# First layer's norm factor applied to products, its inputs split straight from x

## The chip, the cores and the metric

The kernel runs on one core of a Trainium2 chip. The metric is the device time of one execution in microseconds (us). Three runs of the kernel before took 2198.29, 2200.40 and 2200.71 us; the median is 2200.4 us.

## The reference

One layer of a recurrent mixer (with a gated embedding) is followed by one layer that joins a convolution branch, a bidirectional gated recurrence and an MLP. There are 256 tokens of width 2048. The part that matters here is the head of the first layer:

```
def _rmsnorm(x, g):
    xf = x.astype(jnp.float32)
    y = xf * lax.rsqrt(jnp.mean(xf * xf, axis=-1, keepdims=True) + NORM_EPS)
    return (y * g.astype(jnp.float32)).astype(x.dtype)

    u = _rmsnorm(h, norm_pre[i])
...
    proj = u @ w_in
    xb, gate = proj[..., :LRU_WIDTH], proj[..., LRU_WIDTH:]
    xc = conv_general_dilated(xb, conv_w, ...) + conv_b      # 4 taps, causal
    r = sigmoid(einsum(xblk, w_r) + b_r);  i = sigmoid(einsum(xblk, w_i) + b_i)
...
    y = h.astype(u.dtype) * jax.nn.silu(gate)
    return y @ w_out
```

The factor of the norm, `rsqrt(mean(x*x) + eps)`, is one number per token. It is the same for all 2048 features that a product sums over, so it can stand before the product or behind it. The gain `g` is one number per feature and has to stand before it.

## The kernel before, in words

Activations lie with the features on the 128 partitions and the 256 tokens along the row: x is 16 tiles of 128x256. A weight matrix comes as blocks of 128x1024 (512 KB); SyncE loads them in the order of use into a ring of 7 slots, `WF`. Every product is made of three matmuls, so that it keeps f32 precision: ScalarE writes the rounded block, `WH` (a step `high`), VectorE writes what is left, `WL` (a step `low`), and the moving side `SR` is split in the same way. `WH` and `WL` have four slots each: `high` of block n waits until block n-4 has been used. A block is 24 matmuls of 256 columns. Block 0 is the first one that is used; blocks 0 to 7 belong to the first four tiles of the first layer's input projection ("xb" 0 to 3, built side by side, `linear_quad`), and each later tile takes two blocks (`linear`).

All engines walk one list of steps made by `timetable` (L56 to L495); each engine takes from it the steps that concern it, in that order, and waits on semaphores in between. `prepare` puts the `high` steps three blocks (`LA`) ahead of use; a `low` follows at the beginning of the next block. `evac` takes a finished tile out of its PSUM bank (four banks go round), and `after` steps come one, two or three block beginnings later, as the table `AFTER` says. `bg` steps are parts of background work (`small_params`, `recurrence`), one behind every second product.

The start: SyncE loads the parameters (332 KB) and constants, the four pieces of x (512 KB each), then the weights. ScalarE squares the pieces of x, VectorE sums them, TensorE adds over the partitions by a product with ones (`stat`), ScalarE takes the root, VectorE the reciprocal (step `recip`). Only then is x multiplied by gain and factor and split (`normed`, a step `make` for each of the 16 tiles of x).

An xb tile leaves PSUM thus: ScalarE writes it, scaled by the last of the four convolution taps, into `XCf` (L1091), then VectorE adds the other three taps straight from PSUM (L1518 to L1526), and the third of them frees the bank. `after` 1 and 2 split the result for the gates. Tiles of "gates" (sigmoid on ScalarE), and 16 tiles "gate" follow.

Among the weight blocks stand blocks of another matrix, `mod`. The 24 that `add_spread` places are used by TensorE directly, two matmuls of 512 columns each (`modp`), and need neither `high` nor `low`. 14 of them stand among the xb tiles and 10 among the gate tiles. In the middle of the xb tiles VectorE turns masks loaded by DMA into bytes (step `late`).

## Time and profile before

| | before |
|---|---|
| median of three runs | 2200.4 us |
| the profiled execution | 2203.85 us |
| its span, first to last instruction | 2202.1 us |
| mean granted TensorE clock | 0.991 |
| TensorE busy | 2134.1 us (97%) |
| VectorE busy | 1586.3 us (72%) |
| ScalarE busy | 1006.8 us (46%) |
| GpSimd busy | 64.1 us (3%) |

The profiled execution took 3.5 us more than the median. The span leaves out what lies before the first and behind the last instruction, 1.75 us. TensorE is busy for nearly all of the span, so what counts is the time in which it stands still or runs at the lower clock; most of what concerns the change lies in the first 160 us.

### The profile page before, as it was taken

How to read it: one execution, taken by the hardware profiler on the slowest of the kernel's cores; microseconds unless marked ns; L12 is line 12 of the kernel's file. 1: busy time of each engine (PE TensorE's matmuls, PEld its weight loads, DVE VectorE, ACT ScalarE, POOL GpSimd, SP SyncE). 2: the span in 40 equal slices, each digit the busy share in tenths (PEclk: the TensorE clock that was granted, in tenths of full speed). 3: DMA queues.
4: the chain of work that ended last, by engine and by line, in shares of the span. 5: the costliest groups of instructions: out<-in, count | busy, mean ns of one | idle time of the engine just before them, and what ended most of it. 6: DMA issues, size and time to landing. Idle time of an engine off the chain costs nothing.

```text
span 2202.1 us, 34105 instructions
## 1 busy us (share of the span) xinstructions
PE 2134.1 (97%) x14048; PEld 1910.2 (87%) x14048; DVE 1586.3 (72%) x2365; ACT 1006.8 (46%) x1494; POOL 64.1 (3%) x61
## 2 busy tenths in 40 slices
PE   6999999999999999999999999989999999999997
PEld 5877899798988888999999999968888888888885
DVE  6757788588879876567777788776766766656655
ACT  5667444455632322445544444444444434434443
POOL 0000002020000000000000000100000000000011
PEclk9999999999999999999999999999999999999998
DMA  6556777676743466434436988936775675555552
GB/s 227 192 185 203 247 233 274 211 259 210 252 140 124 131 222 240 143 120 127 131 125 198 350 290 297 326 125 199 249 255 185 220 240 192 180 191 191 183 181 87
DMA packets 121691, 447.96 MB, mean 203 GB/s; under 512 B 13504, under 2 KB 13760, under 8 KB 121152
## 3 DMA queue, kind: packets, MB, share of 16 engines
q1 hardware_dynamic: 121536, 445.78, 60.1%
q8 instruction: 111, 1.82, 0.3%
q14 instruction: 44, 0.36, 0.1%
HBM read 441.53 MB, written 4.19 MB: 202 GB/s over the span
## 4 chain that ended last, share of the span: by engine, by line
PE 68%; DVE 4%; ACT 1%; issue 0%; DVEq 0%; ACTq 0%
PE bank L767 67%; DVE AR L1385 1%; DVE WL L1385 1%; DVE AR L1472 1%; DVE AR L1392 1%; DVE SR L1392 0%; PE bank L887 0%; ACT AR L1024 0%; ACT AR L1023 0%; ACT L1024 0%; PE bank L918 0%; ACT WH L1023 0%; ACT SR L1024 0%; DVE SR L1385 0%; ACT SR L1023 0%
## 5 line engine op out<-in xcount | busy, mean ns | idle before, releaser
L767 PE MATMUL bank<-SR,WH 128*128 128x256 f32 (+1 forms) x8128 | 1945.8, 325 | 29.1 <-DVE WL L1385 10.4
L767 PEld LDWEIGHTS bank<-SR,WH 128*128 128x128 f32 x8128 | 1363.5, 191 | 184.6 <-issue 31.0
L767 PE MATMUL bank<-SR,WL 128*128 128x256 f32 (+1 forms) x5088 | 1479.9, 291 | 0.0
L767 PEld LDWEIGHTS bank<-SR,WL 128*128 128x128 f32 x5088 | 972.5, 191 | 14.9
L1385 DVE TENSOR_TENSOR WL<-WF,WH 128x1024 fp32r<-128x1024 f32 x636 | 772.0, 1225 | 218.5 <-ACT WH L1023 218.0
L1023 ACT ACTIVATE WH<-WF 128x1024 fp32r<-128x1024 f32 x636 | 670.7, 1057 | 489.8 <-PE bank L767 448.8
L1392 DVE SCALAR_TENSOR_TENSOR AR<-WF,SM,AR 128x512 f32<-128x512 f32 x345 | 252.3, 752 | 8.7 <-DVE AR L1392 0.9
L1385 DVE TENSOR_TENSOR AR<-AR 128x256 f32<-128x256 f32 (+7 forms) x376 | 167.1, 477 | 60.4 <-ACT AR L1024 37.7
L1023 ACT ACTIVATE AR<-bank 128x256 f32<-128x256 f32 (+2 forms) x199 | 79.8, 415 | 240.1 <-PE bank L767 230.3
L1385 DVE TENSOR_TENSOR AR<-AR,bank 128x256 f32<-128x256 f32 x112 | 47.2, 421 | 120.0 <-PE bank L767 92.6
L1024 ACT ACTIVATE AR<-bank 128x256 f32<-128x256 f32 x152 | 55.7, 380 | 164.0 <-PE bank L767 163.7
L1911 POOL TENSOR_TENSOR AR<-AR 128x256 f32<-128x256 f32 x56 | 63.7, 1137 | 2116.6 <-ACT AR L1024 2116.4
L1023 ACT ACTIVATE SR<-AR 128x256 fp32r<-128x256 f32 (+1 forms) x154 | 62.9, 419 | 102.7 <-DVE AR L1385 83.3
L1385 DVE TENSOR_TENSOR SR<-AR,SR 128x256 fp32r<-128x256 f32 (+1 forms) x154 | 65.6, 435 | 28.0 <-ACT SR L1023 27.4
L1024 ACT ACTIVATE AR<-AR 128x256 f32<-128x256 f32 (+3 forms) x70 | 43.0, 615 | 87.6 <-DVE AR L1385 64.1
L1392 DVE SCALAR_TENSOR_TENSOR AR<-AR,PR 128x256 f32<-128x256 f32 (+12 forms) x168 | 73.8, 442 | 4.8
L767 PE MATMUL bank<-AR 128*128 128x128 f32 (+1 forms) x416 | 65.3, 300 | 9.5 <-ACT AR L1023 8.9
L767 PE MATMUL bank<-WF,SM 128*2 128x512 f32 x160 | 74.3, 601 | 0.0
L767 PEld LDWEIGHTS bank<-AR 128*128 128x128 f32 x416 | 56.9, 194 | 12.4 <-ACT AR L1023 10.4
L1385 DVE TENSOR_TENSOR AR<-bank,AR 128x256 f32<-128x256 f32 x80 | 33.6, 419 | 28.5 <-ACT AR L1024 21.1
L1472 DVE RECIPROCAL AR<-AR 128x256 f32<-128x256 f32 (+1 forms) x12 | 27.4, 2285 | 28.5 <-ACT AR L1024 28.5
L767 PEld LDWEIGHTS bank<-WF,SM 128*2 128x2 f32 x160 | 11.5, 85 | 41.4 <-issue 38.6
(64 smaller groups left out, 463.6 us busy)
## 6 DMA issues: line engine op xcount, KB each, us to landing
WF<-in_mlp SPq DMA_DIRECT2D x256, 512.0 KB, 4.5
WF<-in_mod SPq DMA_DIRECT2D x192, 512.0 KB, 4.8
WF<-in_w_in SPq DMA_DIRECT2D x176, 512.0 KB, 4.3
WF<-in_a_in SPq DMA_DIRECT2D x64, 512.0 KB, 4.9
WF<-in_a_out SPq DMA_DIRECT2D x32, 512.0 KB, 5.5
WF<-in_ple_g SPq DMA_DIRECT2D x32, 512.0 KB, 5.2
WF<-in_w_out SPq DMA_DIRECT2D x32, 512.0 KB, 5.6
WF<-in_pw SPq DMA_DIRECT2D x16, 512.0 KB, 3.6
```

The costliest lines, as they stand in the source:

```text
L767: return tensor.matmul(o, l, r, start=start, stop=stop, skip_group_check=True)
L1023: return scalar.activation(o, x, f, scale=scale)
L1024: return scalar.activation(o, x, f, scale=scale, bias=bias)
L1385: return vector.tensor_tensor(o, a, b, op)
L1392: return vector.scalar_tensor_tensor(o, a, s, b, op1, op2)
L1472: vector.reciprocal(dst, dst).then_inc(st_rs, 1)
L1911: pool.tensor_tensor(ACC, ACC, SQ[ft % 2], ALU.add).then_inc(acc, 1)
```

## The change

The factor of the norm is no longer multiplied into x. `make` now rounds x times gain straight from x on ScalarE, and VectorE writes the rest in one operation; neither needs the factor. The factor is made later (`recip` stands ahead of the last block of the first four tiles), and VectorE multiplies it into each xb and each gate tile as it takes the tile from PSUM: an xb tile into the new area `XB`, where ScalarE and the three taps read it (`after` 1); the split for the gates comes one step later each. The squares of pieces 0 and 1 of x, and all sums, are now GpSimd's; pieces 2 and 3 are squared by ScalarE during the first tiles. SyncE loads the gains (8 KB), then pieces of x and weight blocks by turns, then the other parameters. The step `conditions` (a sigmoid of the conditioning vector, and a multiply) moves from the start to behind the first four tiles. The `mod` blocks stand later: 10 among the xb tiles, beginning with the first gates, and 14 among the gate tiles.

```diff
@@ -50,7 +50,7 @@
-AFTER = {"xb": 2, "gate": 2, "pleg": 1, "cg": 1, "ff": 1, "fb": 1, "gc": 1, "gh": 2, "mlp1": 2}
+AFTER = {"xb": 3, "gate": 2, "pleg": 1, "cg": 1, "ff": 1, "fb": 1, "gc": 1, "gh": 2, "mlp1": 2}
@@ -95,8 +95,7 @@
             add("xb", "a_in", 2 * j + n)
-            add_spread()
-            if j == 2:
+            if j > 2:
                 add_spread()
@@ -279,8 +278,8 @@
-    def begin():
-        prepare()
+    def begin(ahead=LA):
+        prepare(ahead=ahead)
         advance()
@@ -336,14 +335,21 @@
         made = 0
-        for b in range(8):
-            while made < min(2 * b + 2, KT):
+
+        def make(until):
+            nonlocal made
+            while made < min(until, KT):
                 steps.append(("make", kind, made))
                 made += 1
-            begin()
-            while made < min(2 * b + 4, KT):
-                steps.append(("make", kind, made))
-                made += 1
+                if kind == "xb" and made > 8 and made % 4 == 0:
+                    steps.append(("x_square", made // 4 - 1))
+
+        for b in range(8):
+            make(2 * b + 2)
+            begin(min(LA, b + 1) if kind == "xb" else LA)
+            make(2 * b + 4)
+            if kind == "xb" and b == 7:
+                steps.append(("recip", "x"))
             for kk in range(2):
@@ -358,8 +364,12 @@
     steps.append(("start",))
-    prepare(ahead=1)
-    steps.append(("recip", "x"))
+    for q in range(4):
+        steps.append(("load_x", q))
+        steps.append(("load", q))
+        st["issued"] += 1
+    steps.append(("load_params",))
+    prepare(ahead=0)
     seen = set()
@@ -370,6 +380,7 @@
                 linear_quad(kind, j)
+                steps.append(("conditions",))
                 background.append(("small_params", 0))
...
@@ -631,7 +642,7 @@
     UX, UC, UM, DS, PS = split_area(0, 16), split_area(32, 16), split_area(0, 16), split_area(0, 16), split_area(28, 2)
-    XCf, XCs = area(32, 8), split_area(32, 8)
+    XCf, XCs, XB = area(32, 8), split_area(32, 8), area(58, 4)
     RR, II, AA, T2 = area(40, 4), area(44, 4), area(48, 4), area(52, 4)
...
@@ -725,10 +735,15 @@
             if what == "start":
-                sync.dma_start(PR[:, :], ins["params"]).then_inc(s_par, 16)
+                n = PCOL["norm_pre"] + 16
+                sync.dma_start(PR[:, 0:n], ins["params"][:, 0:n]).then_inc(s_gain, 16)
+            elif what == "load_x":
+                q = a[0]
+                sync.dma_start(XT[:, 4 * q:4 * q + 4, :], xv[:, 4 * q:4 * q + 4, :]).then_inc(s_x[q], 16)
+            elif what == "load_params":
+                n = PCOL["norm_pre"] + 16
+                sync.dma_start(PR[:, n:], ins["params"][:, n:]).then_inc(s_par, 16)
                 sync.dma_start(CN[:, :], ins["consts"]).then_inc(s_par, 16)
-                for q in range(4):
-                    sync.dma_start(XT[:, 4 * q:4 * q + 4, :], xv[:, 4 * q:4 * q + 4, :]).then_inc(s_x[q], 16)
             elif what == "load":
...
@@ -1083,12 +1099,14 @@
             ps, leave = psum(what), left(what)[0]
-            w.wait_ge(*full(what))
+            if kind not in ("xb", "gate"):
+                w.wait_ge(*full(what))
             if kind == "xb":
                 w.wait_ge(s_par, 32)
+                w.wait_ge(*left(what))
                 w.wait_ge(xc_lo, j - 7)
                 w.wait_ge(h_done, 4 * (j // 4 - 1))
-                act(XCf[:, j % 8, :], ps, ACT.Identity, scale=par("conv_w", 48 + j), bias=par("conv_b", j)).then_inc(
+                act(XCf[:, j % 8, :], XB[:, j % 4, :], ACT.Identity, scale=par("conv_w", 48 + j), bias=par("conv_b", j)).then_inc(
                     cv_a, 1)
@@ -1097,8 +1115,10 @@
             elif kind == "gate":
+                w.wait_ge(*left(what))
+                w.wait_ge(xc_v, 16)
                 w.wait_ge(ys_lo, j - 1)
-                act(GT[:, 2 + j % 2, :], ps, ACT.Sigmoid).then_inc(ga, 1)
+                act(GT[:, 2 + j % 2, :], GT[:, j % 2, :], ACT.Sigmoid).then_inc(ga, 1)
             elif kind in ("aout", "wout"):
@@ -1169,8 +1189,8 @@
         def after(kind, j, n):
-            if kind == "xb" and n == 1:
-                w.wait_ge(*left((kind, j)))
+            if kind == "xb" and n == 2:
+                w.wait_ge(xc_v, j + 1)
                 if j >= 8:
...
@@ -1369,12 +1389,15 @@
             elif what == "start":
+                w.wait_ge(ones_ok, 1)
+                act(warm[:, 0:1], ONES[:, 0:1], ACT.Sqrt)
+            elif what == "x_square":
+                q = a[0]
+                w.wait_ge(s_x[q], 16)
+                act(BIG[:, 4 * q:4 * q + 4, :], XT[:, 4 * q:4 * q + 4, :], ACT.Square).then_inc(x_sq, 1)
+            elif what == "conditions":
                 w.wait_ge(s_par, 32)
                 act(cs, PR[:, PCOL["c"]:PCOL["c"] + 32], ACT.Sigmoid).then_inc(c_sig, 1)
-                act(warm[:, 0:1], eps, ACT.Sqrt)
-                for q in range(4):
-                    w.wait_ge(s_x[q], 16)
-                    act(BIG[:, 4 * q:4 * q + 4, :], XT[:, 4 * q:4 * q + 4, :], ACT.Square).then_inc(x_sq, 1)
...
@@ -1498,7 +1518,12 @@
         def make(kind, k):
-            if kind != "pleg":
+            if kind == "xb":
+                w.wait_ge(s_gain, 16)
+                w.wait_ge(n_hi, k + 1)
+                stt(UX[:, k, 1, :], XT[:, k, :], par("norm_pre", k), raw(UX[:, k, 0, :]), ALU.mult, ALU.subtract).then_inc(
+                    n_lo, 1)
+            elif kind != "pleg":
                 normed(MAKES[kind], k)
@@ -1513,21 +1538,17 @@
             if kind == "xb":
-                xc = XCf[:, j % 8, :]
-                w.wait_ge(cv_a, j + 1)
-                for tap in (2, 1, 0):
-                    s = 3 - tap
-                    if tap < 2:
-                        marked()
-                    i = stt(xc[:, s:], ps[:, 0:T - s], par("conv_w", tap * 16 + j), xc[:, s:], ALU.mult, ALU.add)
-                    if tap:
-                        mark(i)
-                    else:
-                        i.then_inc(leave, 1)
+                w.wait_ge(*full(what))
+                w.wait_ge(st_rs, RECIP["x"])
+                w.wait_ge(cv_a, j - 3)
+                w.wait_ge(xc_v, j - 3)
+                tt(XB[:, j % 4, :], ps, RX, ALU.mult).then_inc(leave, 1)
             elif kind == "gate":
-                w.wait_ge(ga, j + 1)
-                w.wait_ge(h_done, j + 1)
-                tt(GT[:, j % 2, :], ps, H[:, j, :], ALU.mult).then_inc(leave, 1)
+                w.wait_ge(*full(what))
+                w.wait_ge(cv_a, 16)
+                w.wait_ge(xc_v, 16)
+                w.wait_ge(ys_lo, j - 1)
+                tt(GT[:, j % 2, :], ps, RX, ALU.mult).then_inc(leave, 1)
             elif kind in ("q", "g"):
@@ -1545,11 +1566,28 @@
         def after(kind, j, n):
-            if kind == "xb" and n == 2:
+            if kind == "xb" and n == 1:
+                x, xc = XB[:, j % 4, :], XCf[:, j % 8, :]
+                w.wait_ge(cv_a, j + 1)
+                w.wait_ge(*left((kind, j)))
+                for tap in (2, 1, 0):
+                    s = 3 - tap
+                    if tap < 2:
+                        marked()
+                    i = stt(xc[:, s:], x[:, 0:T - s], par("conv_w", tap * 16 + j), xc[:, s:], ALU.mult, ALU.add)
+                    if tap:
+                        mark(i)
+                    else:
+                        i.then_inc(xc_v, 1)
+            elif kind == "xb" and n == 3:
                 w.wait_ge(xc_hi, j + 1)
                 tt(XCs[:, j % 8, 1, :], XCf[:, j % 8, :], raw(XCs[:, j % 8, 0, :]), ALU.subtract).then_inc(xc_lo, 1)
             elif kind == "gate" and n == 1:
+                w.wait_ge(ga, j + 1)
+                w.wait_ge(h_done, j + 1)
                 w.wait_ge(*left((kind, j)))
+                mark(tt(GT[:, j % 2, :], GT[:, j % 2, :], H[:, j, :], ALU.mult))
+                marked()
                 tt(GT[:, j % 2, :], GT[:, j % 2, :], GT[:, 2 + j % 2, :], ALU.mult).then_inc(gz, 1)
@@ -1883,13 +1921,9 @@
                 vector.tensor_copy(MK[:, :, :], MF).then_inc(mk_ok, 1)
-            elif what == "start":
+            elif what == "conditions":
                 w.wait_ge(c_sig, 1)
                 tt(cf, cs, PR[:, PCOL["c"]:PCOL["c"] + 32], ALU.mult).then_inc(cf_ok, 1)
-                for q in range(4):
-                    w.wait_ge(x_sq, q + 1)
-                    vector.tensor_reduce(XPARTS[:, q, :], BIG[:, 4 * q:4 * q + 4, :].rearrange("p k t -> p t k"), AX_X,
-                                         ALU.add).then_inc(x_part, 1)
             elif what == "finish":
@@ -1904,6 +1938,19 @@
         pool.memset(ONES[:, :], 1.0).then_inc(ones_ok, 1)
+        for q in range(2):
+            w.wait_ge(s_x[q], 16)
+            pool.tensor_tensor(BIG[:, 4 * q:4 * q + 4, :], XT[:, 4 * q:4 * q + 4, :], XT[:, 4 * q:4 * q + 4, :],
+                               ALU.mult).then_inc(p_own, 1)
+        for q in range(4):
+            s = BIG[:, 4 * q:4 * q + 2, :]
+            if q < 2:
+                w.wait_ge(p_own, 2 + q)
+            else:
+                w.wait_ge(x_sq, q - 1)
+            pool.tensor_tensor(s, s, BIG[:, 4 * q + 2:4 * q + 4, :], ALU.add).then_inc(p_own, 1)
+            w.wait_ge(p_own, 3 + q)
+            pool.tensor_tensor(XPARTS[:, q, :], s[:, 0, :], s[:, 1, :], ALU.add).then_inc(x_part, 1)
         for group in range(4):
             for ft in range(1, 15):
                 w.wait_ge(sq, 16 * group + ft + 1)
```

In the lists that follow a row is one or more equal instructions, with the semaphores that it waits for. TensorE, around the last block of the first four tiles; before, the first two `mod` blocks (`WF,SM`) stand in front of it:

```order
L767 MATMUL bank<-WF,SM 2x512 [waits landed3,cf_ok]
L767 MATMUL bank<-WF,SM 2x512
L767 MATMUL bank<-WF,SM 2x512 [waits landed4]
L767 MATMUL bank<-WF,SM 2x512
L767 MATMUL bank<-SR,WH 128x256 [waits n_lo,w_lo]
```

and now the sum over the partitions (`ONES`) stands there:

```order
L782 MATMUL bank<-SR,WL 128x256
L782 MATMUL bank<-AR,ONES 128x256 [waits x_part,ones_ok]
L782 MATMUL bank<-AR,ONES 128x256 [waits x_part] x3
L782 MATMUL bank<-SR,WH 128x256 [waits n_lo,w_lo]
L782 MATMUL bank<-SR,WH 128x256
```

Four `mod` matmuls have gone from this place, and four of ones have come in their stead from the very start of the program.

VectorE, behind the first four tiles; before, three taps for each tile (bank to `AR`), then block 10's `WL`, then small parameters (`SM`):

```order
L1392 SCALAR_TENSOR_TENSOR AR<-bank,PR,AR 128x255 [waits cv_a]
L1392 SCALAR_TENSOR_TENSOR AR<-bank,PR,AR 128x254 [waits v_own]
L1392 SCALAR_TENSOR_TENSOR AR<-bank,PR,AR 128x253 [waits v_own]
L1385 TENSOR_TENSOR WL<-WF,WH 128x1024 [waits w_hi]
L1388 TENSOR_SCALAR SM<-PR 128x16 [waits s_par]
L1385 TENSOR_TENSOR SM<-SM,PR 128x16 [waits v_own]
```

and now:

```order
L1495 RECIPROCAL AR<-AR 128x256 [waits st_sq]
L1408 TENSOR_TENSOR AR<-bank,AR 128x256 [waits st_rs,prod]
L1408 TENSOR_TENSOR AR<-bank,AR 128x256 x3
L1408 TENSOR_TENSOR SM<-SM,PR 128x32 [waits c_sig]
L1408 TENSOR_TENSOR WL<-WF,WH 128x1024 [waits w_hi]
L1415 SCALAR_TENSOR_TENSOR AR<-AR,PR 128x255 [waits free0,cv_a]
L1415 SCALAR_TENSOR_TENSOR AR<-AR,PR 128x254 [waits v_own]
L1415 SCALAR_TENSOR_TENSOR AR<-AR,PR 128x253 [waits v_own]
```

The four multiplies by the factor and the multiply of `conditions` (`SM<-SM,PR`, waits c_sig) stand ahead of block 10's `WL`, and the twelve taps have moved behind it, ahead of the small parameters and of block 11's `WL`.

ScalarE at the same place, now; the table load and the sigmoid of `conditions` stand behind the four tiles:

```order
L1039 ACTIVATE AR<-AR,PR 128x256 [waits free3]
L1039 ACT_TABLE_LOAD
L1039 ACTIVATE SM<-PR 128x32
L1038 ACTIVATE WH<-WF 128x1024 [waits prod,landed4]
L1039 ACT_TABLE_LOAD
L1039 ACTIVATE SM<-SM 128x16 [waits sp_v]
L1038 ACTIVATE WH<-WF 128x1024 [waits prod,landed5]
```

Each of these tiles is now read from `AR` once VectorE has freed its bank (`free3`), and not from the bank.

## Rows read from the trace of the kernel before

**Rows 1.** The page: busy time, share of the span; a group's count, busy us, mean ns.
```profile
PE 2134.1 (97%) x14048; PEld 1910.2 (87%) x14048; DVE 1586.3 (72%) x2365; ACT 1006.8 (46%) x1494; POOL 64.1 (3%) x61
...
L1911 POOL TENSOR_TENSOR AR<-AR 128x256 f32<-128x256 f32 x56 | 63.7, 1137 | 2116.6 <-ACT AR L1024 2116.4
```

**Rows 2.** Timeline, TensorE (start us, us, operation, idle before and its releaser).
```profile
21.57 0.80 PE L767 MATMUL bank<-SR,WH 128*128 128x256 f32 x2 [4.92 <-DVE WL L1385]
...
43.95 3.60 PE L767 MATMUL bank<-WF,SM 128*2 128x512 f32 x8
...
50.33 0.28 PE L767 MATMUL bank<-SR,WL 128*128 128x256 f32 x1
...
52.91 0.47 PE L767 MATMUL bank<-SR,WH 128*128 128x256 f32 x2 [2.30 <-DVE AR L1392]
...
72.98 1.88 PE L767 MATMUL bank<-WF,SM 128*2 128x512 f32 x4
...
75.30 0.47 PE L767 MATMUL bank<-SR,WH 128*128 128x256 f32 x2 [0.44 <-DVE WL L1385]
...
151.77 0.80 PE L767 MATMUL bank<-SR,WH 128*128 128x256 f32 x2 [4.90 <-DVE AR L1392]
```

**Rows 3.** Timeline, DMA issues of SyncE at the start.
```profile
0.74 0.39 SPq L728 DMA_DIRECT2D PR<-in_params  x1
...
1.65 1.85 SPq L731 DMA_DIRECT2D AR<-in_xT  x4
```

**Rows 4.** Timeline, ScalarE at the start: what waits for landings.
```profile
6.54 1.06 ACT L1024 ACTIVATE AR<-AR 128x1024 f32<-128x1024 f32 x1 [0.75 <-DMA AR<-in_xT]
...
8.69 1.06 ACT L1024 ACTIVATE AR<-AR 128x1024 f32<-128x1024 f32 x1 [1.09 <-DMA AR<-in_xT]
...
12.61 1.06 ACT L1023 ACTIVATE WH<-WF 128x1024 fp32r<-128x1024 f32 x1 [0.36 <-DMA WF<-in_a_in]
...
13.90 1.06 ACT L1023 ACTIVATE WH<-WF 128x1024 fp32r<-128x1024 f32 x1 [0.23 <-DMA WF<-in_a_in]
```

**Rows 5.** Timeline, VectorE behind the first four tiles.
```profile
51.25 5.79 DVE L1392 SCALAR_TENSOR_TENSOR AR<-bank,PR,AR 128x255 f32<-128x255 f32 x12 [6.71 <-ACT AR L1024]
...
59.05 0.17 DVE L1388 TENSOR_SCALAR SM<-SM 128x16 f32<-128x16 f32 x1 [0.59 <-ACT SM L1024]
...
62.59 1.22 DVE L1385 TENSOR_TENSOR WL<-WF,WH 128x1024 fp32r<-128x1024 f32 x1
...
63.73 1.43 DVE L1385 TENSOR_TENSOR SR<-AR,SR 128x256 fp32r<-128x256 f32 x4
...
66.46 1.52 DVE L1392 SCALAR_TENSOR_TENSOR AR<-bank,PR,AR 128x255 f32<-128x255 f32 x3
...
72.84 2.35 DVE L1385 TENSOR_TENSOR WL<-WF,WH 128x1024 fp32r<-128x1024 f32 x2
```

**Rows 6.** Timeline, ScalarE behind the first four tiles.
```profile
50.65 1.94 ACT L1024 ACTIVATE AR<-bank,PR 128x256 f32<-128x256 f32 x4 [5.48 <-PE bank L767]
...
73.43 1.28 ACT L1024 ACT_TABLE_LOAD   x1
...
74.73 1.57 ACT L1024 ACTIVATE AR<-bank,PR 128x256 f32<-128x256 f32 x4
```

**Rows 7.** Timeline, GpSimd and VectorE at one moment later.
```profile
342.51 1.77 POOL L1911 TENSOR_TENSOR AR<-AR 128x256 f32<-128x256 f32 x1 [5.49 <-ACT AR L1024]
...
342.47 2.90 DVE L1385 TENSOR_TENSOR WL<-WF,WH 128x1024 fp32r<-128x1024 f32 x2
```

**Rows 8.** Timeline, VectorE and SyncE around the load of the masks.
```profile
139.59 1.52 DVE L1392 SCALAR_TENSOR_TENSOR AR<-bank,PR,AR 128x255 f32<-128x255 f32 x3 [1.22 <-ACT AR L1024]
...
148.19 0.63 DVE L1885 CAST MK<-AR 128x896 uint8<-128x896 f32 x1 [5.95 <-DMA AR<-in_masks]
...
142.64 0.43 SPq L741 DMA_DIRECT2D AR<-in_masks  x1
```

**Rows 9.** Stretch table: us, busy time of PE, PEld, DVE, ACT, POOL; clock, DMA.
```profile
54.00:56.00 2.00, 2.00 (x12) 2.00 (x11) 1.93 (x5) 0.77 (x2) 0.00 (x0) 0.50 0.00 0
```

More of the change, by code:

```diff
@@ L542, in build @@
     landed = [sem(f"landed{i}") for i in range(NF)]
[L543 to L544 removed]
+    s_gain, s_par, s_mk, s_p, s_c, s_keep, s_back, s_out = (
+        sem(n) for n in ("s_gain", "s_par", "s_mk", "s_p", "s_c", "s_keep", "s_back", "s_out"))
     s_x = [sem(f"s_x{q}") for q in range(4)]
@@ L557, in build @@
     sp_v, sp_a, sp_ok = (sem(n) for n in ("sp_v", "sp_a", "sp_ok"))
-    cv_a, xc_hi, xc_lo = (sem(n) for n in ("cv_a", "xc_hi", "xc_lo"))
+    cv_a, xc_v, xc_hi, xc_lo = (sem(n) for n in ("cv_a", "xc_v", "xc_hi", "xc_lo"))
     dec, rc_v, rc_s, h_done = (sem(n) for n in ("dec", "rc_v", "rc_s", "h_done"))
@@ L1480, in low @@
                 w.wait_ge(n_hi, at + k + 1)
-                if sh is None:
-                    tt(S[:, k, 1, :], t, raw(S[:, k, 0, :]), ALU.subtract).then_inc(n_lo, 1)
-                else:
-                    stt(S[:, k, 1, :], t, sh(k), raw(S[:, k, 0, :]), ALU.add, ALU.subtract).then_inc(n_lo, 1)
+                stt(S[:, k, 1, :], t, sh(k), raw(S[:, k, 0, :]), ALU.add, ALU.subtract).then_inc(n_lo, 1)
             w.wait_ge(st_rs, RECIP[stat])
```

22 lines of the change are left out of this document (10 added, 12 removed).

## The prediction

> **What bounds the kernel now.** First the page: TensorE is busy 97% of the span, VectorE 72% [rows 1]. So a change counts by three things: how long TensorE stands still, how long it runs at its lower clock, and what work it is given more. I then went along TensorE's timeline and looked for idle times in brackets. In the stretch that the change touches there are four: it starts only at 21.57, and stands 2.30 at 52.91, 0.44 at 75.30, and 4.90 at 151.77 [rows 2]. After such a pause it is slow: the granted clock is 0.50 in 54 to 56 us, the 1.2 GHz level [rows 9]. What that costs: seven blocks of 24 matmuls lie between 21.57 and 43.95, 22.4 us; at 2.9 for each of the last six the first took 5.0, so a cold start costs 2.1. Two `mod` blocks take 3.60, one 1.8 [rows 2]. Third I asked what ends each pause: each time it is VectorE, with a split or a convolution tap.
>
> I call t0 the moment at which the first four tiles are complete: before, 50.33 + 0.28 = 50.6 [rows 2].
>
> **The start.** SyncE issued 398 KB of parameters ahead of x, and x at 1.65 instead of about 1.15 [rows 3]. The pieces that ScalarE waited for came at 6.54, 8.69, ..., 12.61, 13.90: 2.15 apart, then some 1.3 for each 512 KB [rows 4]. Without the 398 KB (1.0 at that rate) and with the earlier issue (0.5), x's first piece lands at 5.1, and going on in the old spacing the first weight block at 7.2, the second piece at 8.5, the second block at 9.7, the third block 12.4, the fourth 14.9. ScalarE's `high` is 1.06 [rows 4], two makes of 0.4 follow (0.4 is a 256-column pass, 1.57 for four [rows 6]), so at about 8.7 VectorE can begin: two halves of 0.4 and one `WL` of 1.2 [rows 5], and TensorE starts at 10.8.
>
> That is without GpSimd, and here I price an operation that the trace shows only small. At 342.51 a GpSimd add of 256 columns takes 1.77, and the two VectorE splits beside it take 2.90 instead of 2.35 as at 72.84 [rows 5, 7]. The add waited for the first split (to 343.7), worked for 0.55, and the second split waited for it. So they exclude each other, and 256 columns hold VectorE's way for 0.55, 1024 columns for 2.2. The Trainium skill says the same (SBUF — State Buffer, "Who interferes with whom": GpSimd shares one pair of ports with VectorE's second SBUF input, as an exclusive lock); the trace agrees, and by its rule alone the sum would be the one that follows, without it the first rival.
>
> GpSimd squares piece 0 at 5.1 to 7.3, harmlessly, and piece 1 at 8.5 to 10.7, just when VectorE wants its first half. Then they take turns: half to 11.1, sum of 512 columns (1.1) to 12.2, half 12.6, sum (0.55) 13.1, `WL` 14.3. TensorE starts at 14.4, 3.6 later than without GpSimd; I take this. The other end is the mean of 1137 ns for 256 columns [rows 1], which holds waiting too: 4.55 for a square, start at 19.7.
>
> From 14.4: first block cold, 5.0, to 19.4; six more, 17.4, to 36.8. Splits keep up: per block VectorE has 2.0 of work. Then the product with ones. It has left the idle start for the busy path: four matmuls of 256 columns are as many columns as one `mod` block, 1.8, 0.45 each. The last of them needs piece 3: ScalarE's `high` waits for the end of the sixth block (33.9), then 1.06, two makes 0.8, square 1.06: 36.8. GpSimd's two sums 1.65, with a wait behind a split, to 39.0; fourth matmul 39.4; last block: t0 = 42.3. Root and reciprocal (about 2.3) lie beside that block.
>
> Before, t0 was 50.6 with two `mod` blocks done, 47.0 without. The start brings **-4.7** (without GpSimd in the way, t0 = 38.2 and -8.8; at the other end t0 = 47.6 and +0.6).
>
> **Behind t0.** This decides, and VectorE sets it. Now (from t0): four multiplies out of PSUM to 1.5, and bank 0 is free at 0.5, so the pause of 2.30 shrinks to 0.5. But then `conditions`: ScalarE is through with the fourth tile at 2.05 (four take 1.94 [rows 6]), loads a table, 1.28 [rows 6], and the sigmoid comes; VectorE, whose multiply stands ahead of all else, waits till 3.6. `WL` of block 10 to 5.0; twelve taps, 5.7 (5.79 [rows 5]), to 10.7; small parameters: before, from 58.1 (51.25 + 5.79, and a split of 1.14) to 62.59, 4.5, of which 0.59 was a wait for ScalarE at 59.05 that shrinks to 0.2 [rows 5]: to 14.8; `WL` of block 11 to 16.0. TensorE has only blocks 8, 9 and 10 to do, 8.7, and asks for block 11 at 9.2. **It stands 6.8.** Before, the same chain lasted 13.1 (62.59 + 1.14 - 50.6), and TensorE came to block 11 only at 16.1, since it had waited 2.3, was cold and had two `mod` blocks in between: these covered VectorE, and the change has moved them away.
>
> Block 11 is cold, to 21.0. VectorE goes on: small operations 1.3 (between 63.73 + 1.43 and 66.46), multiply 0.4, `WL` 1.15, four halves 1.4 [rows 5], `WL` 1.15 (21.3), taps of tile 4 1.4 (22.7), multiply of tile 5, which frees bank 1, 23.1. Now tile 5's chain with one hop more than before: scaled write and rounding on ScalarE 0.9 and VectorE's half 0.4, taps 1.4 (25.8), rounding 0.4. Only then does ScalarE do a `high` (1.06), a table load (1.28) and the first gate sigmoid: 28.5, bank free at 29.0. TensorE did the first gates block with a short wait for bank 1, and one `mod` block, till 25.8. It stands another 3.2 and then is cold again. Before, sigmoids came at 74.73, t0 + 24.1, and the second gates block at 75.30, t0 + 24.7 [rows 2, 6].
>
> Count without `mod` work: before 24.7 less three blocks (5.4; the third is the 72.98 row, 1.88) is 19.3; now 29.0 less one is 27.2: **+7.9**. The second gates block is cold, before it was not: **+2.1**. The moved `mod` blocks themselves are counted by this; they fall among gate tiles, where TensorE is busy anyway.
>
> **The masks.** Their DMA is issued behind block 32's `WL`, and VectorE waits for it: issue 142.64, landing 148.19, 5.55, and the tap that TensorE waits for follows [rows 2, 8]. Before, that `WL` stood behind tile 12's scaled write (0.6) and taps (1.52 [rows 8]), now behind one multiply of 0.4: 1.7 sooner; behind the landing the chain is 0.3 longer. **-1.4.**
>
> **Other parts**, at nothing: 32 multiplies more on VectorE, 11 us, spread over 200 us in which it has room; shorter parameters load; the longer gate chain, which ends beside products of other tiles, and shows only at the last gate tile (below 0.5).
>
> Sum: -4.7 + 7.9 + 2.1 - 1.4 = **+3.9**. The profiled execution would take 2203.85 + 3.9 = 2207.8. It was 3.5 above the median, so for the median 2200.4 + 3.9 = **2204.3**. Its own range is 2200 to 2209: the pauses could be 2 shorter or longer, a cold stretch 1.5 longer.
>
> **Rivals.**
> *GpSimd is not in the way* (its squares fall between the splits, or x's second piece lands early enough): -8.8 instead of -4.7, 2200.2. For: landings are my extrapolation, and only one operation of 2.2 and two short ones delay the start. Against: rows 7.
> *The start counts in full*, faster: VectorE's backlog does not reach TensorE. Then 4.7 at the start, 1.8 of the 2.30 pause and its cold 2.1, and 1.4 at the masks are gained: 2190.4. For: VectorE is only 72% busy, banks come free by one short operation. Against: the order of the steps; from t0 to block 11's `WL` there are 16 us of chained work against 9.2 of TensorE's. It decides if that chain is below 10.
> *GpSimd holds VectorE for twice as long*, slower: 1137 ns for 256 columns as its real price, t0 = 47.6, +5.3 more, 2209.6. It decides from about 3 us for a square. For: the page's mean. Against: that mean contains waits for VectorE.
>
> **Chances.** A difference of 0.2% (4.4 us) is what a measurement can tell: faster is below 2196.0, slower above 2204.8. My forecast 0.50 (same 0.27, slower 0.23); GpSimd harmless 0.20 (same 0.16, faster 0.03, slower 0.01); start in full 0.13, faster; GpSimd heavy 0.17, slower. Faster 0.16, same 0.43, slower 0.41. The range 2195 to 2210 leaves out most of the fast rival and a little above.
>
> **What would show it.** In the profile after: TensorE's first product near 14.4 (10.8 by the first rival, 19.7 by the last); a VectorE operation lengthened beside a GpSimd square; a pause of 6 to 7 us in TensorE, released by `WL`, some 9 behind t0; VectorE idle for 2 ahead of `SM<-SM,PR`; a second pause of about 3 ahead of the second gates block, released by ScalarE; clock 0.50 after both; a pause of about 3.5 at the masks. I am wrong if TensorE goes through blocks 8 to 12 without a pause.

## The result, and the profile after

The changed kernel takes 2212.9 us, median of 4 runs (2210.2 to 2215.8); the kernel before, run beside it on the same chip, 2199.4 (2196.8 to 2200.7). The ratio is 1.0065, 95% interval 1.0049 to 1.0081: slower by 13.5 us between the medians. Forecast was 2204.3 with a range of 2195 to 2210 (slower 0.41, same 0.43): the time lies above the range.

The profiled execution took 2211.8 us, of which the span is 2210.0 (before 2203.9 and 2202.1). These two single executions lie only 7.9 apart; why, is said below at the mark.

From the profile's page: busy time, and the granted clock in 40 slices of the span, in tenths:

```profile
PE 2130.9 (96%) x14048; PEld 1910.5 (86%) x14048; DVE 1592.2 (72%) x2377; ACT 1006.9 (46%) x1492; POOL 80.2 (4%) x71
...
PEclk9899999999999999999999999999999999999998
```

TensorE's timeline from the start to the first output tiles (start, duration, operation, idle before and what ended it), only rows with an idle time over 0.25:

```profile
14.16 0.80 PE L782 MATMUL bank<-SR,WH 128*128 128x256 f32 x2 [14.16 <-DVE WL L1408]
...
38.60 0.70 PE L782 MATMUL bank<-AR,ONES 128*128 128x256 f32 x2 [1.41 <-POOL AR L1953]
...
42.77 0.47 PE L782 MATMUL bank<-SR,WH 128*128 128x256 f32 x2 [0.61 <-DVE AR L1408]
...
58.76 0.80 PE L782 MATMUL bank<-SR,WH 128*128 128x256 f32 x2 [7.13 <-DVE WL L1408]
...
71.92 0.77 PE L782 MATMUL bank<-SR,WH 128*128 128x256 f32 x2 [2.62 <-DVE WL L1408]
...
149.93 0.80 PE L782 MATMUL bank<-SR,WH 128*128 128x256 f32 x2 [4.99 <-DVE AR L1408]
...
182.27 0.80 PE L782 MATMUL bank<-SR,WH 128*128 128x256 f32 x2 [3.47 <-DVE WL L1408]
...
229.48 0.58 PE L893 MATMUL bank<-CN,AR 2*128 2x2 f32 x4 [2.87 <-ACT AR L1038]
...
318.62 0.51 PE L782 MATMUL bank<-SR,WH 128*128 128x256 f32 x2 [2.35 <-DVE WL L1408]
```

The row at 229.48 is new in such a list: there TensorE transposes a row of modulation sums (`CN,AR`) that ScalarE has copied out of PSUM. I call it **the row**. Against [rows 2] the start is 7.4 sooner, and behind it the idle times are 25.5 us in place of 12.3. The pauses at 182 and 229 lie outside the first 160 us, in which I had looked for most of the effect. Before, the list went on behind 151.77 with 0.91, 0.47, 0.63 and 2.67:

```profile
181.73 0.50 PE L767 MATMUL bank<-SR,WH 128*128 128x256 f32 x2 [0.91 <-DVE WL L1385]
...
299.32 0.50 PE L767 MATMUL bank<-SR,WH 128*128 128x256 f32 x2 [0.47 <-DVE SR L1385]
300.56 0.51 PE L767 MATMUL bank<-SR,WH 128*128 128x256 f32 x2 [0.63 <-DVE SR L1385]
...
303.86 0.80 PE L767 MATMUL bank<-SR,WH 128*128 128x256 f32 x2 [2.67 <-DVE WL L1385]
```

Where the loss ends is read from GpSimd's first sum over an output tile, in which both kernels have done the same work, modulation blocks too. Before and after, each in its own fence:

```profile
312.86 1.39 POOL L1911 TENSOR_TENSOR AR<-AR 128x256 f32<-128x256 f32 x1 [311.92 <-ACT AR L1024]
```

```profile
325.14 0.76 POOL L1958 TENSOR_TENSOR AR<-AR 128x256 f32<-128x256 f32 x1 [286.60 <-ACT AR L1039]
```

It comes 12.3 later, and 200 us further on the distance is still 12.3 (517.63 and 529.93). So the loss has arisen by then. I call this moment **the mark**; every experiment below is read at it, since it is free of what happens by chance in the following 1900 us. That chance is not small: from the mark to its end the profiled execution before took 1889.2 us and the changed one 1884.8, and over the thirteen kernels of this study the same stretch took from 1881.9 to 1891.0. This is why the two profiled executions end only 7.9 apart. The mark is itself a reading of one execution of each kernel, and holds the chance of the slow stretches ahead of it.

A ledger up to the mark: first product -7.4; the product with ones, now on the path, +1.8; idle times +13.1. That is 7.5 of 12.3. The rest is the clock. TensorE's stretches after (us, busy time and count, granted clock, DMA):

```profile
60.00:64.00 4.00, 4.00 (x20) 0.50 0.67 207
...
182.00:186.00 4.00, 3.73 (x17) 0.50 0.64 206
230.00:234.00 4.00, 4.00 (x7) 0.50 0.89 333
```

At 0.50, the 1.2 GHz level, a group of three matmuls (two with `WH`, one with `WL`; a block has eight groups) comes every 0.64 us instead of 0.36. I call such a group slow. Before, about 16 slow groups stand behind the start, after about 28: +3.4. The `mod` blocks' rows add up to 47.9 instead of 46.0 us, +1.9, and the first block has two slow groups fewer, -0.6. Together +4.7, which closes the ledger at 12.2.

### The profile page after: what moved, and what is told of

Its sections match the earlier page's. It is cut to its first block, busy times and chain, and to the rows that moved or that the text cites. A ratio compares the mean times of both kernels' runs of the same rounds, so it can differ in the third digit from the quotient of the medians.

```text
span 2210.0 us, 34193 instructions
## 1 busy us (share of the span) xinstructions
PE 2130.9 (96%) x14048; PEld 1910.5 (86%) x14048; DVE 1592.2 (72%) x2377; ACT 1006.9 (46%) x1492; POOL 80.2 (4%) x71
## 4 chain that ended last, share of the span: by engine, by line
PE 68%; DVE 4%; ACT 1%; issue 0%; DVEq 0%; ACTq 0%
PE bank L782 67%; DVE AR L1408 1%; DVE WL L1408 1%; DVE AR L1495 1%; DVE AR L1415 1%; DVE SR L1415 0%; PE bank L902 0%; ACT AR L1039 0%; ACT AR L1038 0%; ACT L1039 0%; PE bank L933 0%; ACT WH L1038 0%; ACT SR L1039 0%; DVE SR L1408 0%; ACT SR L1038 0%
## 5 line engine op out<-in xcount | busy, mean ns | idle before, releaser
L1408 DVE TENSOR_TENSOR AR<-AR 128x256 f32<-128x256 f32 (+7 forms) x392 | 173.7, 473 | 64.0 <-ACT AR L1039 39.4
L1039 ACT ACTIVATE AR<-bank 128x256 f32<-128x256 f32 x136 | 49.7, 380 | 154.2 <-PE bank L782 154.0
L1039 ACT ACTIVATE AR<-AR 128x256 f32<-128x256 f32 (+3 forms) x84 | 47.5, 567 | 109.7 <-DVE AR L1408 94.6
L1038 ACT ACTIVATE SR<-AR 128x256 fp32r<-128x256 f32 (+1 forms) x138 | 56.6, 420 | 87.8 <-DVE AR L1408 77.2
L1415 DVE SCALAR_TENSOR_TENSOR AR<-AR,PR 128x255 f32<-128x255 f32 (+21 forms) x200 | 89.0, 448 | 5.9
L1408 DVE TENSOR_TENSOR SR<-AR,SR 128x256 fp32r<-128x256 f32 (+1 forms) x138 | 58.9, 435 | 28.9 <-ACT SR L1038 28.8
L782 PEld LDWEIGHTS bank<-AR 128*128 128x128 f32 x416 | 56.2, 192 | 13.9 <-ACT AR L1038 11.8
L1408 DVE TENSOR_TENSOR AR<-bank,AR 128x256 f32<-128x256 f32 x96 | 39.8, 418 | 34.4 <-PE bank L782 27.0
```

The costliest lines, as they stand in the source:

```text
L782: return tensor.matmul(o, l, r, start=start, stop=stop, skip_group_check=True)
L1038: return scalar.activation(o, x, f, scale=scale)
L1039: return scalar.activation(o, x, f, scale=scale, bias=bias)
L1408: return vector.tensor_tensor(o, a, b, op)
L1415: return vector.scalar_tensor_tensor(o, a, s, b, op1, op2)
```

## The experiments

The edits are made in the changed kernel unless said otherwise. The kernel before was measured again beside each group of experiments: 2202.0 beside 1 to 4, 2202.1 beside 5 to 8, 2200.7 beside 9 to 11 (2199.4 beside the changed kernel). So the ratios are to be compared, not the times. The kernel before has its mark at 312.86.

| kernel | median | ratio to before, interval | the mark |
|---|---|---|---|
| changed | 2212.9 | 1.0065, 1.0049 to 1.0081 | 325.14 |
| 1, no wait for the sigmoid | 2209.6 | 1.0039, 1.0025 to 1.0052 | 322.72 |
| 2, small parameters later | 2208.2 | 1.0034, 1.0022 to 1.0046 | 318.80 |
| 3, modulation blocks back | 2200.9 | 0.9994, 0.9985 to 1.0003 | 313.92 |
| 4, squares on ScalarE | 2211.6 | 1.0045, 1.0033 to 1.0057 | 320.94 |
| 5, before, blocks moved | 2204.1 | 1.0004, 0.9994 to 1.0015 | 314.02 |
| 6, chains by steps | 2203.1 | 1.0013, 1.0001 to 1.0026 | 316.22 |
| 7, masks early | 2207.3 | 1.0017, 1.0006 to 1.0029 | 317.22 |
| 8, all edits | 2187.8 | 0.9930, 0.9916 to 0.9945 | 298.30 |
| 9, before, edits 6 and 7 | 2194.0 | 0.9969, 0.9957 to 0.9982 | 304.14 |
| 10, all edits and two | 2179.6 | 0.9911, 0.9897 to 0.9924 | 292.00 |
| 11, x ahead of weights | 2210.6 | 1.0048, 1.0034 to 1.0061 | 323.97 |

### 1: VectorE's wait for the sigmoid

```diff
-            elif what == "conditions":
+            elif what == "conditions_v":
                 w.wait_ge(c_sig, 1)
# timetable, behind the products of tile 4
+            if j == 4:
+                steps.append(("conditions_v",))
```

> The changed kernel with one thing moved: VectorE's product of the condition vector with its sigmoid comes behind tile 4's products instead of right behind the first four tiles, so that VectorE no longer waits there for ScalarE (2.70 us in the changed kernel); ScalarE's sigmoid stays where it is. My theory (VectorE's chain behind t0 sets the pause of 7.13 us ahead of block 11): the pause falls by 2.7 to about 4.4, everything behind it comes 2.7 earlier, and the time falls from 2212.9 to about 2210. Rival (VectorE would only wait at the next step, for tile 0's scaled write): no difference, pause still about 7.

In the changed kernel VectorE's rows behind t0 are these:

```profile
42.20 1.42 DVE L1408 TENSOR_TENSOR AR<-bank,AR 128x256 f32<-128x256 f32 x4 [0.60 <-PE bank L782]
46.31 0.19 DVE L1408 TENSOR_TENSOR SM<-SM,PR 128x32 f32<-128x32 f32 x1 [2.70 <-ACT SM L1039]
46.42 1.22 DVE L1408 TENSOR_TENSOR WL<-WF,WH 128x1024 fp32r<-128x1024 f32 x1
47.55 5.81 DVE L1415 SCALAR_TENSOR_TENSOR AR<-AR,PR 128x255 f32<-128x255 f32 x12
...
57.49 1.22 DVE L1408 TENSOR_TENSOR WL<-WF,WH 128x1024 fp32r<-128x1024 f32 x1
```

With the edit the same `WL` starts at 55.08, though t0 is 0.5 later there, and TensorE:

```profile
56.35 0.80 PE L784 MATMUL bank<-SR,WH 128*128 128x256 f32 x2 [4.24 <-DVE WL L1410]
```

7.13 became 4.24: the wait was on the path. What followed did not all come 2.7 earlier: a wait of 0.63 for tile 5's multiply appeared, and 2.62 became 3.28, since the second gates block hangs on other work (see 3 and 6). The pause at the masks was 3.85 instead of 4.99, and the mark comes 2.4 sooner.

### 2: the small parameters

```diff
-                background.append(("small_params", 0))
# behind tile 5
+            if j == 5:
+                background.append(("small_params", 0))
```

> The changed kernel with the background work on the small parameters begun behind tile 5 instead of behind the first four tiles. My theory: 4.1 us of it lie on VectorE between the twelve taps and block 11's low half, so the pause ahead of block 11 falls from 7.1 to about 3.0, and the time by about 4, to 2209, if the work finds room later (beside tiles 6 and 7). Rival (any work left out here comes back ahead of the gates, where TensorE waits too): pauses ahead of block 11 and of the second gates block still sum to nearly 10, and the time stays at 2212.9.

TensorE's pauses there:

```profile
54.82 0.53 PE L783 MATMUL bank<-SR,WH 128*128 128x256 f32 x2 [2.93 <-DVE WL L1409]
...
65.17 0.48 PE L783 MATMUL bank<-SR,WH 128*128 128x256 f32 x2 [1.05 <-issue]
...
68.44 0.50 PE L783 MATMUL bank<-SR,WH 128*128 128x256 f32 x2 [2.33 <-ACT AR L1040]
```

7.13 became 2.93, as expected. A little of the work came back: ahead of and within the second gates block TensorE now stands 1.05 and 2.33, 3.4 for 2.62, for the small parameters put a short activation with two table loads (1.28 each, at 65.09 and 66.62) between ScalarE's gate sigmoids. At 76 us TensorE is 4.4 ahead of the changed kernel. The mark gains 6.3; most of the difference are shorter slow stretches at 182 and 229, behind the same pauses of 3.48 and 2.87, and these I count as chance.

### 3: the modulation blocks back

```diff
-            if j > 2:
+            for _ in range(1 if j > 2 else 4 * n):
                 add_spread()
```

> The changed kernel with four of the modulation blocks back near the start: they stand between blocks 8 and 9 of the first layer, ahead of block 11, in the number that the kernel before had there. All else stays as changed. My theory (the lost cover costs more than the added multiplies): TensorE has 7.2 us more work ahead of block 11, the pauses of 7.13 and 2.62 go or shrink below 1 together, so do the low-clock stretches behind them, and the row of modulation sums, which stood at 229.5 with a pause of 2.87, is back near 193; the time falls by 10 to 16, to 2197 to 2203. Rival (the added step per tile on VectorE and ScalarE is what costs, wherever the modulation blocks stand): the first pause goes, others of 2 to 5 us come in its place, and the time falls by less than 5.

TensorE behind t0:

```profile
46.51 7.03 PE L782 MATMUL bank<-WF,SM 128*2 128x512 f32 x16 [0.70 <-DVE SM L1408]
...
65.84 0.50 PE L782 MATMUL bank<-SR,WH 128*128 128x256 f32 x2 [1.32 <-DVE AR L1408]
71.90 0.77 PE L782 MATMUL bank<-SR,WH 128*128 128x256 f32 x2 [3.27 <-DVE WL L1408]
```

The 7.03 us of `WF,SM` products stand where the pause was, and it is gone, but for a wait of 1.32 for tile 5's multiply further on; the pause at 229 is gone too. The second gates block starts at 71.90, as without the edit at 71.92: that one does not hang on TensorE's work, and the pause ahead of it is 3.27 instead of 2.62. 11.2 of the 12.3 come back at the mark, and the kernel equals the one before. My expectation that both pauses would go was half wrong, the size of the gain right.

### 4: the squares on ScalarE

```diff
-                if kind == "xb" and made > 8 and made % 4 == 0:
+                if kind == "xb" and made % 4 == 0:
                     steps.append(("x_square", made // 4 - 1))
# GpSimd: no squares, its sums wait for ScalarE's
```

> The changed kernel with the squares of x's first two pieces on ScalarE instead of GpSimd; the sums of squares stay on GpSimd. My theory (a GpSimd square keeps VectorE from its halves of x, 3.35 us for one half in place of 0.44): TensorE's first product comes at about 11 to 12 instead of 14.16, t0 about 3 earlier, all behind it 3 earlier, time about 2210. Rival (the landing of x's second piece at 8.87 or ScalarE's own work sets the start): first product still at 13.5 to 14.2, no difference.

VectorE at the start, in the changed kernel and then with the edit:

```profile
9.09 3.35 DVE L1415 SCALAR_TENSOR_TENSOR SR<-AR,PR,SR 128x256 fp32r<-128x256 f32 x2 [9.09 <-ACT SR L1038]
```

```profile
9.15 0.88 DVE L1415 SCALAR_TENSOR_TENSOR SR<-AR,PR,SR 128x256 fp32r<-128x256 f32 x2 [9.15 <-ACT SR L1038]
...
21.84 3.46 DVE L1408 TENSOR_TENSOR WL<-WF,WH 128x1024 fp32r<-128x1024 f32 x2
```

Two halves take 0.88 without GpSimd beside them and 3.35 with its square (8.87 to 10.76) and the sum behind it (10.84 to 12.16). (My expectation wrote 3.35 for one half; the row is of two.) The ends tell more: in the changed kernel the first half ends at 11.04 and the second at 12.44, each 0.28 behind the end of what GpSimd was doing, so VectorE did not go slower but waited its turn. TensorE starts at 11.22 instead of 14.16. Of these 2.9 only 0.7 are left at t0 (ones at 37.88, before the edit 38.60): I had let the second piece's square slip to 21.3, so its sum came beside two splits, which took 3.46 instead of 2.35, and TensorE stood 1.11 at 26.32; and the first block had more slow groups. The mark gains 4.2, of which 3.5 are shorter slow stretches further back and an idle time at the masks of 4.05 instead of 4.99. That GpSimd keeps VectorE waiting is shown; "all behind it 3 earlier" failed.

### 5: the kernel before, its modulation blocks moved

```diff
-            add_spread()
-            if j == 2:
+            if j > 2:
                 add_spread()
```

> The kernel before with one part of the change alone: the four modulation blocks beside tiles 4 and 5 are taken from there and, as in the changed kernel, follow later (the list of the others moves up). The norm factor, the start and the taps stay as before. My theory (the cover ahead of block 11 is worth as much as it takes VectorE to work off its backlog; without it TensorE waits in the kernel before as well): TensorE comes to block 11 7.2 us sooner, at t0 + 8.9, and VectorE's WL ends at t0 + 13.1: a pause of about 4, a cold stretch behind it, and the row's transposes near 229 with little pause since ScalarE's gate sigmoid does not wait for VectorE there; time + 4 to + 8, some 2207 to 2210 where before is 2202. Rival (the move of the blocks costs nothing by itself): within 2 us of before.

TensorE, from t0 = 45.5 on:

```profile
47.82 0.77 PE L766 MATMUL bank<-SR,WH 128*128 128x256 f32 x2 [2.30 <-DVE AR L1391]
...
58.79 0.50 PE L766 MATMUL bank<-SR,WH 128*128 128x256 f32 x2 [0.66 <-DVE WL L1384]
64.08 0.50 PE L766 MATMUL bank<-SR,WH 128*128 128x256 f32 x2 [2.16 <-DVE WL L1384]
```

My theory failed here, its rival held: the interval of the ratio includes 1, and the mark is 1.2 later. I had forgotten that TensorE keeps its wait of 2.30 for the taps out of PSUM and runs slow behind it, so it asks for block 11 at t0 + 12.6, and the chain ends at t0 + 13.2. Further on 0.44 became 2.16. Moving the blocks costs next to nothing by itself. It costs together with the factor at the evacuation, which frees the bank early (0.61 for 2.30) and, with `conditions`, makes the chain longer (it ends 15.3 + 1.2 behind t0). At the row's products:

```profile
219.29 0.41 PE L877 MATMUL bank<-CN,AR 2*128 2x2 f32 x4 [1.12 <-ACT AR L1022]
```

At the same place of the row this kernel, with the old gate tile, stands 1.12, the changed one 2.87.

### 6: the chains by steps

```diff
-        if first or (kind == "mlp2" and j[1] == 0):
+        if first and kind not in ("gates", "gate") or (kind == "mlp2" and j[1] == 0):
             settle()
```

> The changed kernel with the chains behind tiles 5 and 15 not run through ahead of the first gates block and of the first gate tile, but one step per block, as behind every other tile. My theory: the pause at 182 (3.47, WL of the next block behind the longer chain of tiles 14 and 15) falls to below 1; the pause at 72 (2.62) falls to below 1 as well, since it ends with ScalarE's first gate sigmoid (71.35 to 71.8) and not with VectorE's WL as the profile has it; the low-clock stretch behind 182 goes. Time 4 to 8 less than 2212.9. Rival at 72 (VectorE's WL does end it, as the row says): 2.62 falls only as far as WL comes earlier. Rival at 182: the split of block 40 waits for ScalarE's high part anyway, pause still over 2.5.

Without the edit, VectorE ahead of 182.27:

```profile
176.95 0.40 DVE L1408 TENSOR_TENSOR AR<-bank,AR 128x256 f32<-128x256 f32 x1
178.32 0.42 DVE L1408 TENSOR_TENSOR SR<-AR,SR 128x256 fp32r<-128x256 f32 x1 [0.97 <-ACT SR L1038]
178.66 1.51 DVE L1415 SCALAR_TENSOR_TENSOR AR<-AR,PR 128x255 f32<-128x255 f32 x3
180.66 0.42 DVE L1408 TENSOR_TENSOR SR<-AR,SR 128x256 fp32r<-128x256 f32 x1 [0.48 <-ACT SR L1038]
181.00 2.35 DVE L1408 TENSOR_TENSOR WL<-WF,WH 128x1024 fp32r<-128x1024 f32 x2
```

Two round trips to ScalarE (0.97 and 0.48 of waiting) stand ahead of the split that TensorE wants; before, taps, halves and split followed each other from 178.14 on without a wait over 0.25. With the edit, TensorE:

```profile
70.46 0.47 PE L782 MATMUL bank<-SR,WH 128*128 128x256 f32 x2 [0.94 <-DVE WL L1408]
...
187.03 0.50 PE L782 MATMUL bank<-SR,WH 128*128 128x256 f32 x2 [0.86 <-DVE AR L1408]
```

3.47 became 0.86 and 2.62 became 0.94, as expected; the mark gains 8.9, about 4.9 of it at 182 and 2.6 at 72, slow groups with them. The rest is that no slow stretch follows the row's unchanged pause of 2.87, less one that follows the last gate tile's. What releases the one at 70.46 is told by a ScalarE row and a VectorE row of this kernel, ScalarE first:

```profile
69.89 1.57 ACT L1039 ACTIVATE AR<-bank,PR 128x256 f32<-128x256 f32 x4
```

```profile
68.30 1.23 DVE L1408 TENSOR_TENSOR WL<-WF,WH 128x1024 fp32r<-128x1024 f32 x1 [0.48 <-ACT WH L1038]
```

The split is through at 69.53, the first of the four sigmoids (0.49 each) at 70.38, and TensorE goes on at 70.46: the bank released it, not the `WL` that the row names. In the changed kernel both ended within 0.1 (71.81 and 71.84), and could not be told apart.

### 7: the masks' DMA two tiles earlier

```diff
+            if j == 10:
+                steps.append(("masks",))
...
-            elif what == "late":
+            elif what == "masks":
```

> The changed kernel with the DMA of the masks issued behind tile 10 instead of behind tile 12; VectorE's copy of them stays where it is. My theory: VectorE no longer waits 6.89 us for the landing, the pause of 4.99 at 150 goes, so does the low-clock stretch behind it (6.83 us long, worth up to 3.4): time 5 to 8 less, about 2206. Rival (the taps of tile 12 are late there anyway, or the masks' DMA now delays weight blocks): a pause of 1 or more stays, time less than 3 lower.

The DMA leaves the step `late` for a step `masks` of its own. VectorE's copy of the masks, in the changed kernel and then with the edit:

```profile
146.01 0.63 DVE L1923 CAST MK<-AR 128x896 uint8<-128x896 f32 x1 [6.89 <-DMA AR<-in_masks]
```

```profile
140.40 0.62 DVE L1926 CAST MK<-AR 128x896 uint8<-128x896 f32 x1
```

TensorE has no pause there any more, and my theory held. At the masks alone TensorE gains 7.0: the 4.99, and 2.0 of slow stretch behind. The mark gains 7.9; the rest are slow stretches elsewhere, some shorter and some longer, and a pause of 3.27 for 2.62.

### 8: all edits

> The changed kernel with four things: the modulation blocks back near the start; the chains one step per block; the masks' DMA two tiles earlier; and the squares of x's first two pieces on ScalarE in gaps of its own (piece 0 ahead of the first weight block, piece 1 behind the makes of k-tiles 0 and 1). My theory adds up: the start 2 to 3 earlier (first product at 11.2, without the pause of 1.11 that the first placing of these squares brought), the pauses of 7.13, 2.62, 4.99, 3.47 and 2.87 gone, and most of the cold stretches: about 20 to 25 below the changed kernel, 2188 to 2193, below the kernel before by 9 or more. Rival (VectorE's or ScalarE's work is simply more, and pauses come elsewhere): no lower than 2197.

The edits 3, 6 and 7, and the squares of pieces 0 and 1 on ScalarE in its gaps:

```diff
...
+    steps.append(("x_square", 0))
     prepare(ahead=0)
...
+                if kind == "xb" and (made == 2 or made > 8 and made % 4 == 0):
+                    steps.append(("x_square", made // 4 + (1 if made == 2 else -1)))
```

TensorE starts at 11.04, has the product with ones at 36.35 (so the gain of the start is 2.3 at t0, not 0.7), and has no idle time over 1.5 until the last gate tile, where it stands 2.67 (the largest two between the first and the second of these rows are 1.30 and 0.93):

```profile
36.35 0.70 PE L786 MATMUL bank<-AR,ONES 128*128 128x256 f32 x2 [1.41 <-POOL AR L1950]
...
176.55 0.50 PE L786 MATMUL bank<-SR,WH 128*128 128x256 f32 x2 [0.87 <-DVE AR L1412]
178.42 0.41 PE L897 MATMUL bank<-CN,AR 2*128 2x2 f32 x4 [0.89 <-ACT AR L1042]
```

It beats both kernels, by 0.7% the one before and by 1.3% the changed one.

### 9: the kernel before with the edits 6 and 7

> The kernel before with the two edits that don't belong to the change: the masks' DMA two tiles earlier, and the chains behind tiles 5 and 15 one step per block. It says what of the gain of the kernel with all edits (2187.8 where before is 2202.1) is the change's and what is not. My theory: the pause of 4.90 at 152 and its cold stretch go, 5 to 8 in all, and 0.44 and 0.91 hold little; so 2194 to 2197, and the kernel with all edits is 6 to 9 below that by its earlier start alone. Rival (the norm factor on the products brings nothing even with its side effects mended): this kernel comes to 2190 or less.

2194.0, a gain of 0.31% that has nothing to do with the change. The kernel with all edits is 0.39% below it, 8.6 us, and 5.8 sooner at the mark. So the change is worth some 6 to 9 us once nothing else is late: not as it was written, but with four modulation blocks back near the start and the squares on ScalarE, which is what else tells kernel 8 from this one.

### 10: two edits more

```diff
+        if first and kind == "aout":
+            low_parts()
```

on top of kernel 8, and the small parameters behind tile 5, as in 2.

> The kernel with all edits, and two more: the small parameters begun behind tile 5, and ahead of the first output tile the low half that is due put before the last gate tiles' chains. Theory: of its remaining pauses 1.30 and 0.93 go with the small parameters, and of 2.67 at 290 about half, with the 3.41 of low clock behind it: 2 to 4 below 2187.8. Rival (WH of that block stands behind the table load and the splits on ScalarE, and VectorE's order doesn't matter there): 2.67 stays and the gain is below 1.5.

2179.6, 0.89% below the kernel before. The mark comes 6.3 sooner than in 8, more than I expected: 1.30 and 0.93 became 0.49, and 2.67 became two of 0.40 and 0.66 behind one of 1.08, so that between the start and the mark no slow stretch is left. By the ratios it gains 0.2%, some 4 us, over kernel 8, and the intervals just overlap. It is the fastest kernel of this study. How much these last two edits would give the kernel before was not tried, so the 0.89% is not the change's alone.

### 11: x ahead of the weights

```diff
     for q in range(4):
         steps.append(("load_x", q))
+    for q in range(4):
         steps.append(("load", q))
```

> The changed kernel with x's four pieces issued ahead of the first weight blocks again, as in the kernel before. Theory (the start hangs on the first weight block's landing and its splits): the first block lands 4 to 5 later, near 12, when GpSimd is done with both squares, so its VectorE halves are undisturbed: first product near 15.5 to 16.5 instead of 14.16, t0 later by 1.5 to 2.5, time up by as much. Rival (with the squares out of the way the order of landing makes no difference, since VectorE is what is late): first product within 0.5 of 14.2 and no difference in time.

ScalarE gets the first weight block at 10.68 instead of 7.52, yet TensorE starts at 14.79 instead of 14.16, and the product with ones is 1.3 later. The rival is nearer: with GpSimd's squares in the way, 3.2 us of earlier landing are worth 0.6. The time is even 0.2% lower (1.0048 for 1.0065; the intervals overlap), and at the mark it is 1.2 sooner, with shorter slow stretches. This order is no cause of the loss.

## Why the prediction was wrong, step by step

- **The start**, -4.7: right. First product 14.16 for 14.4, t0 42.16 for 42.3, a term of -4.8. The turns came as written, too: half, sum, half, sum and `WL` ended at 11.04, 12.16, 12.44, 13.02 and 14.11, for 11.1, 12.2, 12.6, 13.1 and 14.3. The reason is shown by experiment 4: VectorE and GpSimd exclude each other here, as [rows 7] had let me see at one moment. That t0 comes out within 0.2 is partly luck: the first block lost less at the lower clock (1.1 for 2.1), and from the last square to the end of the product with ones it took 3.3 for 2.6. The Trainium skill (SBUF — State Buffer, "Who interferes with whom") has it as an exclusive lock; the trace agrees, with 3.35 for 0.88. Of the rivals, "not in the way" would have needed a start at 10.8, and "twice as long" one at 19.7.
- **Behind t0**, +7.9: right in kind and nearly in size. Pauses 7.13 and 2.62 for 6.8 and 3.2; the second gates block at t0 + 29.8 for 29.0, a term of +8.6. Experiments 1 and 2 show two of the chain's members, 3 the cover. The second pause is released by ScalarE's sigmoid, as I had said, though its row names `WL` (6). The sentence that the change "has moved them away" gave only half the cause, as 5 shows: the blocks can be taken away where TensorE is stopped for the taps anyway.
- **Cold behind it**, +2.1: right in kind, five slow groups, +1.4.
- **The masks**, -1.4: wrong. I let the DMA be issued 1.7 sooner and land after the same 5.55. Against the moment at which TensorE stops it was issued 1.2 sooner (5.4 ahead of it for 4.2), and it took 6.5 to land (139.52 to 146.0). The chain behind is 0.3 longer, as written. Measured is 4.99 for 4.90, +0.1. Why the transfer took 0.9 longer no run tells.
- **Other parts, at nothing**: this step failed, and it is most of the miss: +8.5 at two places where I had 0 (the masks add 1.5). I wrote of multiplies "spread over 200 us in which it has room", and "the longer gate chain ... shows only at the last gate tile". VectorE has the room, but two places ask for an order, not for time. I had counted the added hop where the chain of tile 5 is run through at one go, and passed over the same step behind tile 15. At 182, where the chains of tiles 14 and 15 are run through at one go, each hop added to a chain is a round trip ahead of TensorE's next split: 3.47 for 0.91, and eight slow groups, 2.2, together +4.8 (experiment 6). At 229 ScalarE's copy of the row stands behind the rounding of a gate tile's product, a gate sigmoid and a `high`. The rounding waits 3.79 for VectorE's two gate products, and these stand behind four sums of 2.73: 2.87 where there was no pause, and three slow groups, together +3.7. Of the pause 1.12 goes with the row's new position alone (5). The other 1.75 I put down to the longer gate chain, by comparison with 5: there is one product more between the sums and the rounding (0.88 for 0.42), and the sums start only 2.9 ahead of TensorE's stop for 4.1. No run takes this place apart by itself; with the blocks back the row meets the gate tiles elsewhere and the pause is gone (3).

That place in the changed kernel: ScalarE's rounding, sigmoid and copy, and then VectorE's rows, of which the second is what the rounding waits for:

```profile
227.25 0.42 ACT L1038 ACTIVATE SR<-AR 128x256 fp32r<-128x256 f32 x1 [3.79 <-DVE AR L1408]
227.59 0.42 ACT L1039 ACTIVATE AR<-AR 128x256 f32<-128x256 f32 x1
...
228.86 0.57 ACT L1038 ACTIVATE AR<-bank 2x512 f32<-2x512 f32 x1
```

```profile
223.69 2.73 DVE L1415 SCALAR_TENSOR_TENSOR AR<-WF,SM,AR 128x512 f32<-128x512 f32 x4
226.34 0.88 DVE L1408 TENSOR_TENSOR AR<-AR 128x256 f32<-128x256 f32 x2
```

The terms as measured: -4.8 + 8.6 + 1.4 + 0.1 + 4.8 + 3.7 = 13.8. At the last gate tile, where I had a loss below 0.5, there is a gain (2.35 with no slow stretch, for 3.77 with nine slow groups), -3.9, and the slow `mod` blocks are +1.9: 11.8, where the mark says 12.3 and the forecast +3.9. These last two I had not looked for. The nine slow groups of before at 303.86 are partly chance: kernels 3, 5, 8 and 9 have five or six behind a pause of the same 2.67.

What stays open: the medians lie 13.5 apart, the mark 12.3 and the two profiled executions 7.9. One us is within what a slow stretch more or less makes, and no run here tells it.

## What to carry to other kernels

A factor that is taken from the operands and applied to the products starts the products earlier, but it adds a hop to every tile's way out of PSUM. Price the hop not by its 0.4 us in the engine's free time, but at each place where a chain is run through at one go, or where another engine's copy stands behind it, and let no split that TensorE wants stand behind such a chain. Filler work that hid a backlog has to stay beside it when an edit makes the backlog longer; and an earlier start shows its worth (here 6 to 9 us, with the modulation blocks back and the squares on ScalarE) only when the next thing that is late has been mended as well.
